# Latent queries of three token tiles computed beside the first attention steps instead of in the expansion stage, and a split router shift row

## The reference

```
q_mla = einsum('btr,re->bte', rmsnorm(cq, g_qa), w_uq)      # 256 -> 8 * 96
q_mla = concat([q_mla[..., :64], axial_rope(q_mla[..., 64:])])   # latent tokens only
k, v  = mla_expand(ckv, kpe, w_ukv)                          # 128 -> 8 * (64 + 64)
o_mla = softmax(q_mla k^T * MLA_SCALE) v                     # context tile: own 128 keys; latent tiles: 640 keys
h2 = rmsnorm(x) * (1 + sc2) + sh2
router logits = h2 @ w_router                                # 24 columns: so the shift sh2 gives one row sh2 @ w_router
```

## Time and profile before

| | |
|---|---|
| runs | 1337.52, 1341.08, 1343.81 us; median 1341.08 |
| profiled execution | span 1336.3 us from the first to the last instruction; the page gives no separate total for it |
| PE busy | 1279.6 us (96%) |
| DVE, ACT, POOL busy | 613.7, 358.8, 152.5 us (46%, 27%, 11%) |
| granted PE clock, mean | 0.991 of full |

### The profile page before, as it was taken

The page is one execution under the profiler, slowest core; times in us unless marked ns, Lnnn a source line. Parts: engine busy times, 40 slices in busy tenths (PEclk is TensorE's granted clock), DMA queues, the critical chain, the costliest instruction groups (busy, mean ns, idle before and its releaser), DMA issues. The chain is left out here.

```text
span 1336.3 us, 17216 instructions
## 1 busy us (share of the span) xinstructions
PE 1279.6 (96%) x6042; PEld 735.3 (55%) x6042; DVE 613.7 (46%) x1519; ACT 358.8 (27%) x931; POOL 152.5 (11%) x257
## 2 busy tenths in 40 slices
PE   6999999999999999999999999989999999999997
PEld 3555555565666564444455555566666656444443
DVE  0132266444566463433343224655556536344438
ACT  1121255434343210000012114563444311100001
POOL 2210220000000110000142003000000011000014
PEclk9999999998999999999999999999899999999999
DMA  9976996499111489999694038430201139999966
GB/s 355 363 248 220 347 332 254 162 359 327 42 64 64 168 333 398 361 374 367 260 334 161 16 140 291 151 128 15 88 33 64 63 130 352 404 368 360 362 270 246
DMA packets 125441, 313.16 MB, mean 234 GB/s; under 512 B 9882, under 2 KB 58426, under 8 KB 112688
## 3 DMA queue, kind: packets, MB, share of 16 engines
q1 hardware_dynamic: 90896, 243.13, 49.8%
q0 software_dynamic: 12848, 45.39, 9.0%
q10 hardware_dynamic: 21616, 23.60, 5.3%
HBM read 232.14 MB, written 80.71 MB: 234 GB/s over the span
## 5 line engine op out<-in xcount | busy, mean ns | idle before, releaser
L790 PE MATMUL ps<-ring,big 128*128 128x384 f32 (+2 forms) x640 | 230.7, 520 | 1.7 <-DVE big L1773 1.3
L790 PEld LDWEIGHTS ps<-ring,big 128*128 128x128 f32 x640 | 120.3, 190 | 104.6 <-issue 63.7
L871 PE MATMUL ps<-ring,arena 128*128 128x512 f32 x384 | 169.3, 594 | 1.9 <-ACT arena L1406 1.9
L502 PEld LDWEIGHTS ps<-consts,arena 128*128 128x128 f32 (+2 forms) x880 | 103.7, 143 | 79.1 <-issue 50.9
L502 PE MATMUL ps<-consts,arena 128*128 128x128 f32 (+2 forms) x880 | 129.7, 278 | 15.7 <-ACT arena L1227 6.6
L711 PE MATMUL ps<-ring,big 128*128 128x512 f32 x320 | 143.0, 598 | 0.8
L563 PE MATMUL ps<-arena 64*128 64x128 f32 (+5 forms) x576 | 137.9, 430 | 6.1 <-DVEq L1822 3.4
L1227 ACT ACTIVATE arena<-ps 128x384 f32<-128x384 f32 (+3 forms) x140 | 69.1, 493 | 221.3 <-PE ps L502 221.3
L871 PEld LDWEIGHTS ps<-ring,arena 128*128 128x128 f32 x384 | 71.2, 190 | 83.1 <-issue 83.1
L563 PEld LDWEIGHTS ps<-arena 64*128 64x128 f32 (+1 forms) x576 | 79.4, 196 | 65.8 <-issue 57.8
L711 PEld LDWEIGHTS ps<-ring,big 128*128 128x128 f32 x320 | 59.0, 190 | 70.4 <-issue 66.4
(11 more groups left out here) (237 smaller groups left out, 1481.9 us busy)
## 6 DMA issues: line engine op xcount, KB each, us to landing
ring<-in_w_mod SPq DMA_DIRECT2D x40, 1024.0 KB, 11.8
ring<-in_w_up SPq DMA_DIRECT2D x22, 1024.0 KB, 9.7
ring<-in_w_gate SPq DMA_DIRECT2D x22, 1024.0 KB, 7.6
slots<-zeros ACTq DMA_DIRECT2D x8, 2560.0 KB, 14.4
slots<-zeros SPq DMA_DIRECT2D x8, 2560.0 KB, 20.2
arena<-in_w_down SPq DMA_DIRECT2D x16, 1024.0 KB, 12.7
arena<-slots SPq DMA_DIRECT2D x30, 512.0 KB, 6.4
slots<-arena POOLq DMA_DIRECT2D x30, 512.0 KB, 9.6
```

What stands on the lines that cost most here:

```text
L502: return pe.transpose(out, in_, ident)
L790: mm = pe.matmul(ps[:, c, 0:CHUNKS[c][1]], hT[:, s, k, :], slot[c][:, k, 0:CHUNKS[c][1]], start=(k == 0), stop=(k == KD - 1))
L871: mm = pe.matmul(ps[:, b, :], xgT[:, b, k * P:(k + 1) * P], w_gu[q][:, :, k, :], start=(k == 0), stop=(k == KD - 1))
```

## The change

Queries of the context tile and of latent tile 0 stay in the expansion stage (`EARLY = 2`). For the other three tiles a table `BESIDE` names a job for half-steps of latent attention: `uqA` and `uqB` make 512 and 256 of the 768 query columns, `qtA` and `qtB` transpose four heads each. All of them, and the router shift row (`bw`, now at step 5, second half), go through lane M, bank 7. ACT copies `uqA`, `uqB` and `qtA`, DVE rotates after `uqB` and copies `qtB`. `qt` moves to the buffer `mrow`. The two `spin` calls of step 0 are gone. The shift row is made for both kinds of token in two column halves of the array. SP loads `xh` only after the last `uqB`, since it now overlaps `cqT`.

```
+EARLY = 2
+BESIDE = {(0, 0): ("uqA", 2), (0, 1): ("uqB", 2), (1, 0): ("uqA", 3), (1, 1): ("uqB", 3),
+          (2, 0): ("qtA", 2), (2, 1): ("qtB", 2), (3, 0): ("qtA", 3), (3, 1): ("qtB", 3),
+          (4, 0): ("uqA", 4), (4, 1): ("uqB", 4), (5, 1): ("bw", 0), (6, 0): ("qtA", 4), (6, 1): ("qtB", 4)}
...  PE, shift_logits
-                for kind in range(2):
-                    for k in range(KD):
-                        mm = pe.matmul(ps[:, 7, kind * RW:(kind + 1) * RW], modc2[:, kind, 0, k:k + 1].broadcast_to([P, P]),
+                for k in range(KD):
+                    for kind in range(2):
+                        mm = pe.matmul(ps[64 * kind:64 * kind + 64, 7, 0:RW], modc2[:, kind, 0, k:k + 1].broadcast_to([P, 64]),
...  PE, new: one job for half-step (s, h)
+            def late_query(L, s, h):
+                what, i = BESIDE.get((s, h), (None, 0))
+                if what == "bw":
+                    shift_logits(L)
+                if what in ("uqA", "uqB"):
+                    n, w = {"uqA": (0, 512), "uqB": (512, 256)}[what]
+                    t = ORDER[i]
+                    M.take(pe, (what, L, i))
+                    for k in range(2):
+                        mm = pe.matmul(ps[:, 7, 0:w], cqT[:, k, t * P:(t + 1) * P], wuq[:, k, n:n + w],
...
+                if what in ("qtA", "qtB"):
+                    h0 = {"qtA": 0, "qtB": 4}[what]
+                    M.take(pe, (what, L, i))
+                    pe.wait_ge(q_done, TILES * L + i + 1)
...  PE, latent attention
                                 scores(s, (h,))
-                                if s == 0:
-                                    spin(7, 2)
+                            late_query(L, s, h)
                             if turning:
                                 turn(s - 3, h)
...  PE, ACT, DVE, expansion stage
-                    if i < TILES:
+                    if i < EARLY:
...  SP
+                            row_load(rowB2[0], 3, 0, rows_in)
+                            sp.wait_ge(M.full, M[("uqB", L, LAST)])
+                        sp.dma_start(xh, src[t * P:(t + 1) * P, half * 512:(half + 1) * 512]).then_inc(xh_in, 16)
...  ACT, after exps(s, h)
+                            late_query(L, s, h)
...  DVE, shift_logits
+                for kind in range(2):
+                    src = ps[kind * half:(kind + 1) * half, 7, 0:RW]
+                    for at in (0, half):
+                        last = TT(bwr[at:at + half, kind, :], src, cst["pad"][kind * half:(kind + 1) * half], ALU.add)
...  DVE, new
+                if what == "uqB":
+                    dve.wait_ge(M.free, M.freed[(what, L, i)])
+                    rope_query(L, i)
+                if what == "qtB":
+                    t0 = ORDER[i] * P
+                    dve.wait_ge(M.full, M[(what, L, i)])
+                    dve.tensor_copy(qT[0:QK, 4:8, t0:t0 + P],
...  DVE, after maximum(s, h) and copy(s - 3, h)
+                        if phase == 4:
+                            late_query(L, s, h)
```

More of the change, by code:

```diff
@@ L240, in program @@
         v_mla, A3 = place(o, KVT, 512)
-        qt, o = place(A3, 2, 768)
-        rq, o = place(o, 2, 256)
+        qt = mrow[:, :, :].rearrange("p a b -> p (a b)").rearrange("p (a b) -> p a b", a=2)
         pb4 = ring[:, 0:5120].rearrange("p (a b n) -> p a b n", a=DEEP, b=2)
@@ L245, in program @@
         pt4 = [[pt4a[:, 0], pt4a[:, 1]], [pt4a[:, 2], pt4a[:, 3]]]
+        rq, _ = place(o, 2, 256)
         h2T, o = place(o, D)
@@ L258, in program @@
         gi, ei = r_gi.bitcast(U32), r_ei.bitcast(U32)
-        rowG1, o = place(0, 2, D)
-        xh, o = place(o, 512)
-        r_lg, o = place(o, TILES, RW)
+        xh, o = place(0, 512)
+        rowG1_latent, o = place(2 * TOK, D)
+        r_lg, o = place(2 * D + 512, TILES, RW)
         r_g8, o = place(o, TILES, 8)
@@ L1252, in attention, with late_query @@
                         beside(L, s)
+            def late_query(L, s, h):
+                what, i = BESIDE.get((s, h), (None, 0))
+                if what in ("uqA", "uqB"):
+                    n, w = {"uqA": (0, 512), "uqB": (512, 256)}[what]
+                    act.wait_ge(M.full, M[(what, L, i)])
+                    if what == "uqA":
+                        if i - 2 < EARLY:
+                            act.wait_ge(S[i % 2].full, S[i % 2][("qt", L, i - 2)])
+                        else:
+                            act.wait_ge(M.full, M[("qtB", L, i - 2)])
+                    act.activation(qt[:, i % 2, n:n + w], ps[:, 7, 0:w], ACT.Copy, scale=MLA_SCALE).then_inc(M.free, 1)
+                if what == "qtA":
+                    t0 = ORDER[i] * P
+                    act.wait_ge(M.full, M[(what, L, i)])
+                    act.activation(qT[0:QK, 0:4, t0:t0 + P], ps[0:QK, 7, :].rearrange("p (h n) -> p h n", h=4),
+                                   ACT.Copy).then_inc(M.free, 1)
             def beside(L, s):
@@ L1698, in shift_logits, with rope_query, late_query @@
                 dve.wait_ge(M.full, M[("bw", L)])
-                then(dve, "dve", TT(bwr[:, :, :], ps[:, 7, 0:2 * RW].rearrange("p (a b) -> p a b", a=2),
-                                    cst["pad"].unsqueeze(1).broadcast_to([P, 2, RW]), ALU.add))
-                dve.sem_inc(M.free, 1)
+                half = P // 2
+                for kind in range(2):
+                    src = ps[kind * half:(kind + 1) * half, 7, 0:RW]
+                    for at in (0, half):
+                        last = TT(bwr[at:at + half, kind, :], src, cst["pad"][kind * half:(kind + 1) * half], ALU.add)
+                then(dve, "dve", last)
+                dve.sem_inc(M.free, 1)
+            def rope_query(L, i):
+                t = ORDER[i]
+                x = qt[:, i % 2, :].rearrange("p (h d) -> p h d", h=MLA_H)[:, :, NOPE:QK]
+                dve.wait_ge(q_done, TILES * L + i)
+                t1 = rq[:, 0, :].rearrange("p (h d) -> p h d", h=MLA_H)
+                t2 = rq[:, 1, :].rearrange("p (h d) -> p h d", h=MLA_H)
+                TT(t1, x, c32[:, t, :].unsqueeze(1).broadcast_to([P, MLA_H, ROPE]), ALU.mult)
+                for ax in range(2):
+                    for j in range(2):
+                        o0, i0 = 16 * ax + 8 * j, 16 * ax + 8 * (1 - j)
+                        last = TT(t2[:, :, o0:o0 + 8], x[:, :, i0:i0 + 8],
+                                  s32[:, t, o0:o0 + 8].unsqueeze(1).broadcast_to([P, MLA_H, 8]), ALU.mult)
+                then(dve, "dve", last)
+                TT(x, t1, t2, ALU.add).then_inc(q_done, 1)
+            def late_query(L, s, h):
+                what, i = BESIDE.get((s, h), (None, 0))
+                if what == "bw":
+                    shift_logits(L)
+                if what == "uqB":
+                    dve.wait_ge(M.free, M.freed[(what, L, i)])
+                    rope_query(L, i)
+                if what == "qtB":
+                    t0 = ORDER[i] * P
+                    dve.wait_ge(M.full, M[(what, L, i)])
+                    dve.tensor_copy(qT[0:QK, 4:8, t0:t0 + P],
+                                    ps[0:QK, 7, :].rearrange("p (h n) -> p h n", h=4)).then_inc(M.free, 1)
             def blend(L, i, a, b):
```

50 lines of the change are left out of this document (19 added, 31 removed).

## The result

| | before | after |
|---|---|---|
| median of the runs | 1339.73 us (1337.52 to 1343.81, 4 runs) | 1350.56 us (1349.19 to 1351.58, 4 runs) |
| profiled span | 1336.3 us | 1348.8 us |
| after / before | | 1.0075, 95% interval 1.0056 to 1.0095 |

What follows compares the result with a forecast made beforehand. PE, busy 96% of the span, bounds the kernel. Steps 0 to 6 +13.3 and +10.4, lag +1.0, expansion -15.0 give +9.7; clock falls +4.1 make +13.8 on 1341.1: 1355 us, range 1340 to 1362.

Steps and rivals of the forecast that it cites:

- rival 1: Latent attention: waits as worked out but the clock stays up, +9.7 us, 1351 us; chance 15%.
- Expansion stage: First matmul to first scores: 23.3 us instead of 30.8, gaining 7.5 per layer, with new waits before `uk`.
- Steps 0 to 3: Start of latent attention: ends at 16.8 us instead of 9.35, 8.0 of it PE idle, waiting on bank 7's copies.
- The longest wait: Before `qtB` 2: PE idle 3.0 us for a copy behind DVE's rotation, normalising, maximum and ACT's exponential.
- Steps 4 to 6: Latent attention with 512-column scores: 4.1 us of waits left, as larger scores cover more; shift row taken as 2.0 us.
- The clock: Thin stretch in steps 2 to 4: a short fall to half clock, +4.1 us for both layers.
- Lag at step 7: After steps 0 to 6: ACT and DVE running behind adds 0.5 us per layer.
- The later load of `xh`: SP's load after the last `uqB`: 0 to 3 us if late, taken as 0.
- 10.1 us: Low-clock stretches before the change: loss of 6.7 and 3.4 us in the two layers, assuming work there takes twice as long.
- (4): Long fall of the clock in both layers: +18 us, 1359 us; chance 10%.
- (2): Faster: bank 7 waits half as long and clock up, -8 us, 1333; decides from 7.3 us idle per layer downward; chance 12%.
- Rival 3: No tellable change: waits a quarter to a third shorter, clock falls once, about +3 us, 1344; chance 13%.

Runs made afterwards that it cites:

- e4: Changed kernel plus multiplications of zeros into an unread bank, placed in PE's waits of steps 0 to 3: 1344.43 us, ratio 1.0036 to the kernel before.
- e3: Changed kernel with DVE's rotation of the three late query tiles left out: 1343.14 us, ratio 1.0027 to the kernel before.
- e2: Changed kernel with `uqB` and `qtB` of tiles i = 2 and 3 moved to bank 3 with own semaphores: 1338.03 us, ratio 0.9987 to the kernel before.
- e7: Kernel before with the old wide shift row moved to step 5, all queries in their old place: 1346.06 us, ratio 1.0046 to the kernel before.
- e10: Changed kernel with a second bank for late jobs and four multiplications of zeros in step 2: 1335.76 us, ratio 0.9985 to the kernel before.
- e8: Kernel before with the two-half shift row at step 5 and one multiplication of zeros in each of steps 1 and 2: 1329.95 us, ratio 0.9932.
- e5: Changed kernel with the old wide shift row back in step 1, so only the queries move: 1356.99 us, ratio 1.0142 to the kernel before.
- e1: Kernel before with only the shift row changed, two halves at step 5, queries unmoved: 1335.11 us, ratio 0.9967 to the kernel before.
- e6: Kernel before with the shift row in two halves but still at step 1: 1333.93 us, ratio 0.9964 to the kernel before.

## Why the prediction was right

The forecast was slower by 13.8 us with a short fall of the clock in each layer; 10.8 came, by that mechanism. The time alone wouldn't show it: 1350.56 us lies just outside the forecast's own 1351 to 1359, and nearer to rival 1 (1351, the clock stays up). Added to the later median of the kernel before, 1339.73, the 13.8 us would be 1353.5. It is the granted clock in the trace that decides between the two. And the terms hit less well than their sum, since two misses were of opposite sign. e4, with the clock up, is measured for them, from the start of one PE job to the start of the next, as the forecast counted; a bracket is some 0.17 us shorter than a wait counted so. Step by step:

- **Expansion stage.** Forecast 23.3 us, waits of 1.3 and 1.7 us before `uk`: 23.41, 1.11 and 1.53.
- **Steps 0 to 3.** Forecast 16.8 us at full clock: e4 has its first big scores 16.0 us after the first scores. The waits, zeros included, are 6.6 us where 8.0 were forecast; PE's own work is 9.4 us where 8.8 were. The longest wait was forecast at 3.0 us, with this chain, and is 2.36 in the bracket, 2.5 counted as the forecast did. e3 shows DVE's rotation in the chain, e2 the shared bank.
- **Steps 4 to 6.** Forecast 17.3 us (34.1 - 16.8): 16.3 in e4. Here the waits are 2.8 us, forecast 4.1. The shift row takes 1.0 us to the next start, forecast 2.0: it had been scaled by a half from the old row. The rest of PE's work takes 12.5 us, forecast 11.2, most of the difference in the turned probabilities and values (2.1 for 1.3).
- **Luck.** Per layer the waits were 2.7 us too large and the row 1.0, and the rest of PE's work 1.9 too small. With PE's other work priced right the forecast would have been 13.8 + 2 x 1.9 = 17.6 us, further from the result.
- **The clock.** A fall in steps 2 to 4 of each layer, of 6.8 us, costing 2.0: it begins at the end of step 2, lasts 6.6 and 6.8 us and costs 2.2. That it hangs on the thin stretch is shown by e4. The Trainium skill (TensorE: Matmul & The Clock Gate, "A second HAM failure mode: psum-queue depth-cycling") ties swings of the clock to PE standing idle briefly and often between groups of matmuls that cycle through PSUM banks. The trace agrees: PE waits often, 0.25 to 2.36 us, between groups that share one bank, and the clock falls in both layers. Frequent waits alone are not enough: e3 has them too, 0.25 to 1.24 us in steps 0 to 3, and the clock stays up there.
- **Lag at step 7.** Forecast 0.5 us per layer: none. Before and after stand 3.19 us apart at step 7 of layer 0 and 3.06 at scores some 88 us later (403.56 before, 406.62 after):

```profile
406.62 1.33 PE L589 MATMUL ps<-arena 96*128 96x512 f32 x4
```

  The later load of `xh`, priced at 0, lies in this stretch and costs nothing either.
- **What no step had.** The rest of layer 0 takes 0.9 us longer, all of it after 450 us, and that of layer 1 takes 2.0. The third fall is 1.7 of it, and e7 shows it without the late queries. What remains is within what the profiles differ by: without a fall there, the rest of layer 0 takes 586.6 to 588.1 us, with the queries late (e10, 586.6) or not (before 586.6, e8 588.1); the changed kernel has 587.4.

The sum in these terms, for both layers: forecast 9.7 + 4.1 = 13.8. The expansion stage came 0.1 per layer higher, the waits 2.7 lower, the row 1.0 lower, PE's other work 1.9 higher, lag 0.5 lower, the fall 0.2 higher: 13.8 + 2 x (0.1 - 2.7 - 1.0 + 1.9 - 0.5 + 0.2) = 9.8, which is the sum of the stages in the profile (3.4 + 6.4). The rivals: the clock stays up (1) is what e4 builds, and it needs zeros for it; of a long fall (4) there is no trace; that the waits would be half as long (2) is refuted by 9.4 us against 12.1, where it decided from 7.3 on downward (the trace of the changed kernel has 7.4, counted by the ends of records and with the low clock in it). Rival 3 had the waits about right (22% shorter), but not PE's other work nor the clock, which fell in both layers.

What the prediction didn't ask is what the two parts do apart. It credited the low clock of before, which its stage times contain, to the change as a whole. e5, with the queries moved and the wide row kept, still has the long low stretch; e1's profile, with the row's part alone, has none, and that kernel is faster. The size of it, 10.1 us, was also misread: half of the low stretches would be lost only if the slower work filled no waits of PE. e7 has the same wide row, at another step and at full clock, and takes 19.07 us in both layers against 23.75 and 20.84, so the low clock cost about 4.7 + 1.8 = 6.5 us. The sum of the forecast doesn't use the 10.1.

The zeros of step 0, which the change drops, were not tested alone.

## What to carry to other kernels

Work moved beside other work isn't hidden when it shares a bank and the engines of its copies with it: here three tiles of queries saved 7.4 us in their old place and cost over 15 in the new one (32.4 against 17.1 us at full clock), since each job waited for a copy that stood behind maxima and exponentials. A second bank and zeros (e10) still left 3.8 us per layer of it. Split a change into its parts before judging it: one part of this one gains 0.33%, and the other hides it. Check the terms of a forecast and not only its sum: here waits priced too high and work priced too low nearly met. Where the clock falls in some executions and not in others, look for thin stretches of PE and fill their waits with multiplications of zeros, which cost nothing in e4 and e8.

## What the runs showed of the hardware

- 32 matmul records with 24 columns of data, weights 128 wide, take 3.65 us; with weights 64 wide, for the two halves of the array in turn, 1.12 us: a factor of 3.3, not 2. The median weight load goes from 190 to 137 ns, which is not enough by itself; how much the two halves overlap was not measured apart.
- The clock fell before the change although PE was busy in 6.27 of 6.30 us, and in the changed kernel after 9.03 busy of 13.20. A busy share doesn't tell which; in e1's profile, with 15.13 of 17.10, it stayed up.
- One kernel's executions differ by about 1%, and their mean granted clock with them: e1 by 11 us, e7 by 14, e6 by 15.5 (1330.03 us at 0.997 to 1345.57 at 0.984). The same 20 records took 1.31 us in one profile and 2.40 in another, at code that the kernels share. A single profile of such a kernel may show a fall that most runs don't have, or miss one that most have.
